# The HGRN scan of a two-layer encoder: seven of its eight score levels as 32 by 32 blocks instead of 64 by 64, and ScalarE placing more of them

## What is computed

```
z = h @ w_in ; q, f_fwd, f_bwd, i, gate = split(z)        # 5 x 1024 columns, 8 heads of 128
q = silu(q) ; f = lb + (1 - lb) * sigmoid(f_logit) ; k = 1 - f ; g = log(f)
per chunk (forward in time, and again backward), b = cumsum(g):
  scores[t, s] = sum_d q[t, d] k[s, d] exp(b[t, d] - b[s, d])   for s <= t, else 0
  o = scores @ v + (q * exp(b)) @ S
  S = exp(b_last) * S + (k * exp(b_last - b)).T @ v
o = rms_norm(o_fwd + o_bwd) * silu(gate) ; out = o @ w_out
```

## Time and profile before

| | us |
|---|---|
| median of three runs (2829.45 to 2836.46) | 2833.17 |
| the profiled execution | 2831.86 |
| its span | 2830.1 |
| PE busy / DVE / ACT / POOL | 2742.6 / 1369.5 / 729.7 / 920.0 |

### The profile page before, as it was taken

How to read it: one execution, slowest core, us unless ns; L and a number is a source line. 1 busy time by engine, 2 the same in 40 slices (tenths; PEclk the granted TensorE clock), 3 DMA queues, 4 the chain that set the end, 5 groups by cost and what they waited for, 6 DMA issues and landing times.

```text
span 2830.1 us, 40126 instructions
## 1 busy us (share of the span) xinstructions
PE 2742.6 (97%) x16781; PEld 2467.6 (87%) x16781; DVE 1369.5 (48%) x1563; ACT 729.7 (26%) x1016; POOL 920.0 (33%) x403
## 2 busy tenths in 40 slices
PE   7998999999999999999999999999989999999998
PEld 6887998999999999999888888888868888888887
DVE  6287887442212322235777676778563223222234
ACT  3015887121100011003233334334231000110003
POOL 2230001334433444333322232224334344443441
PEclk9998999999999999999999999999999999999999
DMA  4010000111111111112111111112111111111111
GB/s 155 23 38 8 0 0 8 45 45 45 49 49 45 46 45 45 48 57 100 31 38 31 31 31 38 31 31 83 38 38 52 46 45 52 44 44 52 45 50 70
DMA packets 178223, 125.40 MB, mean 44 GB/s; under 512 B 4914, under 2 KB 171140, under 8 KB 178086
## 3 DMA queue, kind: packets, MB, share of 16 engines
q1 hardware_dynamic: 176790, 118.60, 13.8%
q10 hardware_dynamic: 1296, 4.73, 0.4%
HBM read 114.93 MB, written 8.39 MB: 44 GB/s over the span
## 4 chain that ended last, share of the span: by engine, by line
PE 86%; DVE 7%; issue 4%; ACT 3%; DMA 0%; ACTq 0%; SPq 0%; DVEq 0%
PE ps L1317 74%; PE ps L1443 3%; PE ps L1571 2%; PE ps L1536 1%; DVE ssq L884 1%; ACT prob L610 1%; PE ps L1393 1%; DVE tmp L892 1%; PE ps L1610 1%; ACT kk L705 1%; PE ps L1411 1%; PE ps L1548 0%; DVE y L959 0%; PE ps L1585 0%; DVE amax L1005 0%
## 5 line engine op out<-in xcount | busy, mean ns | idle before, releaser
L1317 PE MATMUL ps<-xh,wsp 128*128 128x512 f32 (+2 forms) x4864 | 1125.9, 356 | 17.3 <-DVE xl L878 12.7
L496 POOL TENSOR_TENSOR wsp<-raw,ones 128x1024 fp32r<-128x1024 f32 x198 | 379.7, 1918 | 1851.5 <-PE ps L1317 1832.9
L1317 PEld LDWEIGHTS ps<-xh,wsp 128*128 128x128 f32 x4864 | 839.7, 189 | 108.0 <-issue 21.3
L1317 PE MATMUL ps<-xl,wsp 128*128 128x348 f32 (+2 forms) x2432 | 617.1, 351 | 0.0
L1317 PE MATMUL ps<-ah,wsp 128*128 128x348 f32 (+2 forms) x2560 | 567.0, 350 | 0.0
L498 POOL TENSOR_TENSOR wsp<-raw,wsp 128x1024 fp32r<-128x1024 f32 x198 | 531.4, 2684 | 15.5
L1317 PEld LDWEIGHTS ps<-ah,wsp 128*128 128x128 f32 x2560 | 443.1, 188 | 44.7
L1317 PEld LDWEIGHTS ps<-xl,wsp 128*128 128x128 f32 x2432 | 430.4, 189 | 44.2
L655 ACT ACTIVATE tmp<-tmp 128x1044 f32<-128x1044 f32 (+1 forms) x64 | 68.5, 1070 | 1097.7 <-DVE tmp L1055 557.1
L1317 PE MATMUL ps<-al,wsp 128*128 128x348 f32 (+1 forms) x1280 | 322.5, 349 | 0.0
L1317 PEld LDWEIGHTS ps<-al,wsp 128*128 128x128 f32 x1280 | 225.2, 188 | 23.2
(11 more groups left out here) (199 smaller groups left out, 2799.5 us busy)
## 6 DMA issues: line engine op xcount, KB each, us to landing
raw<-in_w SPq DMA_DIRECT2D x128, 512.0 KB, 3.9
raw<-in_c_w_in SPq DMA_DIRECT2D x40, 512.0 KB, 3.8
raw<-in_ab_w_in SPq DMA_DIRECT2D x12, 512.0 KB, 3.8
xst<-in_x SPq DMA_DIRECT2D x8, 512.0 KB, 6.8
raw<-in_ab_w_out SPq DMA_DIRECT2D x8, 512.0 KB, 4.1
h_kept<-h ACTq DMA_DIRECT2D x8, 512.0 KB, 2.6
h<-h_kept SPq DMA_DIRECT2D x8, 512.0 KB, 5.9
out<-ost SPq DMA_DIRECT2D x16, 256.0 KB, 3.1
```

The source lines that it names most:

```text
L496: nc.gpsimd.tensor_tensor(wsp[:, slot, 0, :], raw[:, slot, :], one, ALU.mult).then_inc(w_high, 1)
L1317: ins = M(ps[:, 3 * s + c, 0:n], w(a, k), b(k)[:, c0:c0 + n], start=(k == first and a == 0 and b is xa), stop=(k == last and a == 1))
```

## The change

- `level`: levels 0 to 6 are made as 32 by 32 blocks: 32 products per level instead of 16, each with 32 keys as weights and 32 queries streamed. The block of tokens c goes to output partitions 32 (c mod 4) to 32 (c mod 4) + 31, so four neighbouring blocks of a chunk fill its four quarters, in a strip of 32 columns per chunk. Levels 0 to 5 lie inside the 32-blocks; level 6 is the pair of the two 32-blocks of a 64-block, as level 7 is of the 64-blocks. Level 7 is as it was.
- `merge`: only levels 0 to 5, and over 8 strips of 32 columns; for levels 6 and 7 DVE waits for the level and copies nothing.
- `place` becomes `place_near` (four copies of 32 partitions by 256 from `ac`, after merge 5), `place_far` with 32 (four copies of 32 by 256 from bank 6, after level 6) and `place_far` with 64 (the two copies of level 7, as before). The first two stand ahead of the wait for level 7 in ACT's list. Ten copies are counted where four were.
- `k_turn` waits for all ten copies (before: seven merges and two of the four copies); `o_products` for all ten.
- The masks are loaded for 6 levels by 32 columns, by four DMAs of 32 partitions instead of two of 64.

```diff
-HB = 64
+HB, QB = 64, 32
...
-            for b in range(2):
-                part = slice(HB * b, HB * (b + 1))
-                nc.sync.dma_start(mskf[part], masks[part, 0:7, part]).then_inc(s_msk, 16)
+            for b in range(4):
+                part = slice(QB * b, QB * (b + 1))
+                nc.sync.dma_start(mskf[part], masks[part, 0:6, part]).then_inc(s_msk, 16)
...
-            def place(hd):
-
-                aa = aas[hd % 2]
-                act.wait_ge(h_lv, 8 * hd + 8)
-                for b in range(2):
-                    part, far = slice(HB * b, HB * (b + 1)), slice(HB * (1 - b), HB * (2 - b))
-                    A(aa[part, :, far], ps[part, 7, :].rearrange("p (a b) -> p a b", b=HB), ACT.Copy).then_inc(h_aa, 1)
-                act.wait_ge(h_le, 7 * hd + 7)
-                for b in range(2):
-                    part = slice(HB * b, HB * (b + 1))
-                    A(aa[part, :, part], ac[part], ACT.Copy).then_inc(h_aa, 1)
+            def place_near(hd):
+
+                act.wait_ge(h_le, 6 * hd + 6)
+                for b in range(4):
+                    part = slice(QB * b, QB * (b + 1))
+                    A(aas[hd % 2][part, :, part], ac[part], ACT.Copy).then_inc(h_aa, 1)
+
+            def place_far(hd, size):
+
+                act.wait_ge(h_lv, 8 * hd + (7 if size == QB else 8))
+                bank = ps[:, 6 if size == QB else 7, 0:8 * size].rearrange("p (a b) -> p a b", b=size)
+                for b in range(P // size):
+                    part, far = slice(size * b, size * (b + 1)), slice(size * (b ^ 1), size * ((b ^ 1) + 1))
+                    A(aas[hd % 2][part, :, far], bank[part], ACT.Copy).then_inc(h_aa, 1)
...
                 pair_keys(hd, 7)
+                place_near(hd)
+                place_far(hd, QB)
                 if not nxt:
                     gate_o(7)
-                place(hd)
+                place_far(hd, HB)
...
                 dve.wait_ge(h_lv, 8 * hd + (lv + 1))
-                if lv == 7:
+                if lv >= 6:
                     return
...
-                bank = ps[:, 6 + lv % 2, :].rearrange("p (a b) -> p a b", b=HB)
-                V.copy_predicated(ac[:], msk[:, lv:lv + 1, :].to_broadcast([P, 8, HB]), bank).then_inc(h_le, 1)
+                bank = ps[:, 6 + lv % 2, 0:8 * QB].rearrange("p (a b) -> p a b", b=QB)
+                V.copy_predicated(ac[:], msk[:, lv:lv + 1, :].to_broadcast([P, 8, QB]), bank).then_inc(h_le, 1)
...
-                for c in range(16):
-                    t0, b = N_META + c * HB, c % 2
+                size = HB if lv == 7 else QB
+                for c in range(SEQ // size):
+                    t0, b, chunk = N_META + c * size, c % (P // size), c * size // P
                     if lv == 0:
-                        left, right = zf[:, 1, t0:t0 + HB], zq[:, t0:t0 + HB]
-                    elif lv < 7:
-                        left, right = kp[:, t0:t0 + HB], paired(qqs[hd % 2], t0, HB, LEVELS[lv - 1])
+                        left, right = zf[:, 1, t0:t0 + size], zq[:, t0:t0 + size]
+                    elif lv < 6:
+                        left, right = kp[:, t0:t0 + size], paired(qqs[hd % 2], t0, size, LEVELS[lv - 1])
                     else:
-                        far = t0 + HB - 2 * HB * b
-                        left, right = kp[:, t0:t0 + HB], qqs[hd % 2][:, 1 - b, far:far + HB]
-                    ins = M(ps[HB * b:HB * (b + 1), 6 + lv % 2, (c // 2) * HB:(c // 2 + 1) * HB], left, right, start=True, stop=True)
+                        far = N_META + (c ^ 1) * size
+                        left, right = kp[:, t0:t0 + size], qqs[hd % 2][:, 1 - b % 2, far:far + size]
+                    ins = M(ps[size * b:size * (b + 1), 6 + lv % 2, chunk * size:(chunk + 1) * size], left, right, start=True, stop=True)
...
                 if half == 0:
                     pe.wait_ge(h_uk, 7 * hd + 7)
-                    pe.wait_ge(h_le, 7 * hd + 7)
-                    pe.wait_ge(h_aa, 4 * hd + 2)
+                    pe.wait_ge(h_aa, 10 * hd + 10)
```

More of the change, by code:

```diff
@@ L161, in encoder @@
         ol7 = at("ol7", [P, SEQ], F32R, o_k + 4096)
-        mskf = at("mskf", [P, 7, HB], F32, o_k)
+        mskf = at("mskf", [P, 6, QB], F32, o_k)
         st = at("st", [P, 8, P], F32, o_k + 8192)
@@ L165, in encoder @@
         stb = at("stb", [P, 8, P], F32, o_t + 2 * row)
-        msk = at("msk", [P, 7, HB], U8, o_c + 1484 + 72)
+        msk = at("msk", [P, 6, QB], U8, o_c + 1484 + 72)
         dec = at("dec", [P, 2, 8], F32, e_c)
-        ac = at("ac", [P, 8, HB], F32, e_c + 64)
-        e_c = e_c + 64 + 2048
+        ac = at("ac", [P, 8, QB], F32, e_c + 64)
+        e_c = e_c + 64 + 1024
         kept = nc.dram_tensor("h_kept", (KT, P, SEQ), F32, kind="Internal").ap()
@@ L1126, in merge @@
                 dve.wait_ge(h_lv, 8 * hd + (lv + 1))
-                if lv == 7:
+                if lv >= 6:
                     return
                 if lv == 0 and hd:
-                    dve.wait_ge(h_aa, 4 * hd)
+                    dve.wait_ge(h_aa, 10 * hd)
                 elif lv:
-                    dve.wait_ge(h_le, 7 * hd + lv)
-                bank = ps[:, 6 + lv % 2, :].rearrange("p (a b) -> p a b", b=HB)
-                V.copy_predicated(ac[:], msk[:, lv:lv + 1, :].to_broadcast([P, 8, HB]), bank).then_inc(h_le, 1)
+                    dve.wait_ge(h_le, 6 * hd + lv)
+                bank = ps[:, 6 + lv % 2, 0:8 * QB].rearrange("p (a b) -> p a b", b=QB)
+                V.copy_predicated(ac[:], msk[:, lv:lv + 1, :].to_broadcast([P, 8, QB]), bank).then_inc(h_le, 1)
             def halves(a, t0, n, m):
@@ L1249, in _ @@
             store_real(zq[:], 2)
-            dve.wait_ge(s_msk, 32)
+            dve.wait_ge(s_msk, 64)
             V.tensor_copy(msk[:], mskf[:]).then_inc(h_mk, 1)
@@ L1525, in o_products @@
                 pe.wait_ge(h_ch, hd + 1)
-                pe.wait_ge(h_aa, 4 * hd + 4)
+                pe.wait_ge(h_aa, 10 * hd + 10)
                 pe.wait_ge(z_free, E_HG + hg(min(hd + 1, 7), 0) + 1)
@@ L1558, in level @@
                 if lv > 1:
-                    pe.wait_ge(h_le, 7 * hd + (lv - 1))
+                    pe.wait_ge(h_le, 6 * hd + (lv - 1))
                 elif hd:
                     pe.wait_ge(h_de, 4 * hd + (lv - 1))
-                for c in range(16):
-                    t0, b = N_META + c * HB, c % 2
+                size = HB if lv == 7 else QB
+                for c in range(SEQ // size):
+                    t0, b, chunk = N_META + c * size, c % (P // size), c * size // P
                     if lv == 0:
-                        left, right = zf[:, 1, t0:t0 + HB], zq[:, t0:t0 + HB]
-                    elif lv < 7:
-                        left, right = kp[:, t0:t0 + HB], paired(qqs[hd % 2], t0, HB, LEVELS[lv - 1])
-                    else:
-                        far = t0 + HB - 2 * HB * b
-                        left, right = kp[:, t0:t0 + HB], qqs[hd % 2][:, 1 - b, far:far + HB]
-                    ins = M(ps[HB * b:HB * (b + 1), 6 + lv % 2, (c // 2) * HB:(c // 2 + 1) * HB], left, right, start=True, stop=True)
+                        left, right = zf[:, 1, t0:t0 + size], zq[:, t0:t0 + size]
+                    elif lv < 6:
+                        left, right = kp[:, t0:t0 + size], paired(qqs[hd % 2], t0, size, LEVELS[lv - 1])
+                    else:
+                        far = N_META + (c ^ 1) * size
+                        left, right = kp[:, t0:t0 + size], qqs[hd % 2][:, 1 - b % 2, far:far + size]
+                    ins = M(ps[size * b:size * (b + 1), 6 + lv % 2, chunk * size:(chunk + 1) * size], left, right, start=True, stop=True)
                 ins.then_inc(h_lv, 1)
```

## The result

The changed kernel takes 2803.43 us (median of four runs, 2799.07 to 2805.14), the kernel before 2831.55 beside it (2829.45 to 2836.46): 28.1 us less, a ratio of 0.990 with a 95% interval of 0.9883 to 0.9918. That is outside the predicted range (2806 to 2865), and 2.6 us under the time that the second rival gave (2806). The profiled execution took 2804.8 us, its span is 2803.0.

What follows compares the result with a forecast made beforehand. PE was taken to bound the kernel. Levels at +5.0 and waits at -6.0 summed to -1.0 us, giving 2830.9 for the profiled execution and 2832.2 for the median; the forecast was 2831.5 us, range 2806 to 2865.

Steps and rivals of the forecast that it cites:

- the second rival: PE's levels 0 to 6: four matmuls overlap on four output quarters; -26 us in all, 2806; chance 0.14.
- What bounds the kernel: Whole kernel: PE, busy 97% of the span; other engines' savings count only where PE waits for them.
- Levels 0 to 6: PE's 56 levels: 64 records of 32 columns take 1.02 us, +0.09 us a level, +5.0 us in all.
- the line through the earlier trace: PE's float32 matmul price, fitted to 512 and 128 columns: 0.829 ns per column plus 5.4 ns.
- two at a time: PE in levels 0 to 6: two 32-column matmuls overlap and take 31.9 ns, so a level takes 1.02 us.
- the lower end: PE's levels 0 to 6 with all four array quarters running together: 0.51 us a level, -24 us.
- Level 1: PE's level with single-element query reads, 1.48 us: same +0.09 us as the other levels.
- The rule that speaks against the change: Skill pages on PE: matmul starts never closer than about 25 ns; 1.6 us a level, +37 us before waits.
- The wait before level 7: PE waiting for DVE's join_queries: narrower merges save 0.9 of 0.99 us in six heads, -5.4; head 7 -0.6.
- ACT's placing: ACT's eight new copies, 0.35 us each, 2.8 us together, end before level 7 comes and are free.
- Small edits: Other merges, bank 6, DVE's empty waits: 0; mask DMAs hidden, at most +1.4 once; mask cast at most -0.3.
- The sum: Whole kernel: +5.0 for the levels and -6.0 for the waits make -1.0 us; forecast 2831.5.

Runs made afterwards that it cites:

- the run on one half: The kernel before with each level's 16 products reordered, eight of the lower half of the output partitions, then eight of the upper: 2873.4 us.
- the two fastest kernels: The changed kernel with all sums of squares cut into four quarters, 2788.0 us; the same with DVE's o_gate moved behind level 6's joins in heads 0 to 6, 2782.6 us.

## Why the prediction was wrong

**What bounds the kernel: right.** PE held the chain before and after, and every gain is time that PE no longer spends or waits.

**Levels 0 to 6: the step that failed.** The prediction had the price of one matmul right, 31.9 ns for 32 columns from the line through the earlier trace rows; on one quarter it is 31.7. It had the number at a time wrong. It kept "two at a time" for blocks that go round four quarters and made +5.0 us of it; four are at a time, and a level takes 0.57 us from first to last start where the prediction had 1.02 and the lower end 0.51. Against four at a time the text argued that each product is two matmuls on the same quarter, so that in order only neighbours overlap. The mean spacing of the kernel before fits that argument as well as it fits two halves always at work, so it could not decide. Its single starts could. If the two matmuls of a product stood next to each other on one half, the first record of a level would start alone, and pairs would follow. In the kernel before the first two matmuls of the level at 1564.81 start 6 ns apart and their weight loads 7; in the run on one half they are 107 and 55 ns apart. So the first pair is already one matmul on either half, and with four quarters in turn the first four start within 20 ns. The 2 of the kernel before was the number of parts that the order visited, not a depth of overlap. How two matmuls of one product come to stand apart, the trace doesn't say. The run with two quarters in turn shows what the prediction had costed: 0.92 us a level, where it had 1.02, and 2822.5 us.

In numbers: the 56 levels, with entry and exit, save 0.39 x 6 + 0.67 = 3.0 us a head, 24.1 in eight, in place of +5.0. The lower end of the term, -24, was right, and was given a chance of 0.14; the rival's time came out near because both of its terms did (-24 and about -2, against -24.1 and -2.8).

**Level 1: mis-sized.** It was given the same change as the others. It took 1.48 and takes 0.81: its extra of 0.40 us falls to 0.12. The slow single-element reads, too, go on in four quarters, as its times on one, two and four quarters show.

**The rule that speaks against the change.** No start-to-start floor near 25 ns shows across quarters: records are 8.9 ns apart on average, and some 7. On one quarter the spacing is 31.7 ns, above the floor that "TensorE: Matmul & The Clock Gate" of the Trainium skill states (its section on the 56 ns gap), so for one part of the array the rule isn't tested here. What "TensorEngine Tiling (Array Packing)" of the Trainium skill says under Theoretical Speedup, up to 4 times for a dimension of 32 or less, is what the order of the blocks shows up to its loosened ends: 1.72 us on one quarter, 0.92 on two, 0.57 on four.

**The wait before level 7: the mechanism right, the size off.** DVE is ready 13.74 - 12.86 = 0.88 us earlier after level 5; 0.62 to 0.94 was forecast. But level 6 brings PE there 0.39 us earlier, not 0.09 later, so 0.49 us of the stop is left where 0 to 0.28 was forecast. Six heads gave 2.9 us where the sum had 5.4. In head 7 nothing was gained: its stop before level 4 went from 1.07 to 1.15 where 0.6 less was forecast, and no run takes that stop apart. In all 2.8 us of waiting went where the sum had 6.0. Rival 2 had this as its own remark (0.3 x 7).

**ACT's placing: right, with a thinner cover.** The four copies from `ac` take 0.43 us each (1.72 for four) and those from bank 6 a median of 0.38, not 0.35. They no longer end before level 7; ACT goes on without a pause and ends at 1564.37, 2.65 us before k_turn. Taken out of their cover they cost k_turn 0.4 us a head.

**Small edits: right.** No new wait at k_turn, and none of SP's. A merge of 256 columns takes 0.46, as forecast.

**The sum.** From the start of the scan's first level to the sums of the norm behind the mixer the stretch is 24.8 us shorter (2102.14 - 1355.62 before, 2074.77 - 1353.09 after): 1.8 in head 0, 21.0 in heads 1 to 6, and 2.0 from head 7 on. The terms above, 24.1 and 2.8, make 26.9; a lower clock in head 0 took 1.4 back (below), and waits on DVE and "issue" around the last head most of the rest. Another 2.5 us between the two profiled spans lie ahead of the scan, in code that the change leaves alone (but for the masks). They are no effect of it that the runs show: in eight further profiled executions, whose code ahead of the scan is that of one of the two kernels, the scan starts anywhere from 1348.9 to 1355.5 us.

## What to carry to other kernels

When small products go to different 32- or 64-column parts of the output partitions, count the parts that the order visits in turn, and divide: the time is the price on one part over the number of parts, here 31.7 ns on one quarter and some 8 to 9 with four. The order of issue is then worth as much as the shape. The same holds for matmuls that load many weight columns and stream few, such as sums with a vector of ones: cut into four quarters they took 0.64 us instead of 1.68. And look at single starts before settling on how many matmuls overlap: a mean spacing fits more than one story.

## What the runs showed that I had not expected

- The order on the array is loose: near a change of quarter, matmuls for the next quarter seem to start among the last of the old one, for some eight records (1.72 us for what would be 2.04).
- In head 0, which has no stop before level 7, the gain was 1.8 us, though its levels alone save 3.4 (its level 0 went from 1.83 to 1.08 us). PE had just stood still for 3.7 us, and its clock was at the lower level (0.50, 1.2 GHz). In the kernel before it rose soon after; in the changed one it was at 0.50 for longer, and the 27 projection matmuls behind level 0 took 6.73 us instead of 5.29. Granted clock is the column behind the busy times, before and after, from the start of level 0:

```profile
1355.60:1358.60 3.00, 2.98 (x36) 2.87 (x37) 1.11 (x2) 0.00 (x0) 0.00 (x0) 0.54 0.00 1
1358.60:1361.60 3.00, 3.00 (x19) 3.00 (x18) 0.80 (x2) 0.00 (x0) 0.00 (x0) 0.89 0.00 0
```
```profile
1353.10:1356.10 3.00, 3.00 (x71) 2.94 (x72) 1.63 (x3) 0.00 (x0) 0.00 (x0) 0.50 0.03 5
1356.10:1359.10 3.00, 3.00 (x12) 3.00 (x11) 0.00 (x0) 0.00 (x0) 0.00 (x0) 0.50 0.00 0
```

The shape of level 0 doesn't decide it. In the run with the late copies head 0 begins with the same 64 records behind the same stop of 3.7 us, and the clock was back earlier:

```profile
1353.38:1356.38 3.00, 3.00 (x71) 2.94 (x72) 1.63 (x3) 0.00 (x0) 0.00 (x0) 0.55 0.03 7
1356.38:1359.38 3.00, 3.00 (x18) 3.00 (x18) 0.00 (x0) 0.00 (x0) 0.00 (x0) 0.88 0.00 0
```

There level 0 and the 27 matmuls behind it take 0.95 and 5.74 us, 6.7 together, against 7.8 in the changed kernel; the runs with the old merges, with half of the columns and with the output's sums in quarters have 6.7 to 6.8 too, and the two fastest kernels 7.8 and 7.4. What decides it from one execution to the next, no run here tells.
